# A query projection split around the first cross-attention scores, with an order of its own for ScalarE, in a two-layer decoder trunk

## The reference, cut to what matters

```
def memory_cross_attention(h, mem_n, wq, wkv, qn_g, kn_g, wo):
    B, S, _ = h.shape
    q = rmsnorm((h @ wq).reshape(B, S, XA_HEADS, XA_HEAD_DIM), qn_g)
    k, v = jnp.split(mem_n @ wkv, 2, axis=-1)
    k = rmsnorm(k.reshape(B, MEM_LEN, XA_HEADS, XA_HEAD_DIM), kn_g)
    ...
    s = jnp.einsum("bshd,bmhd->bhsm", q, k).astype(jnp.float32) * (XA_HEAD_DIM ** -0.5)
    p = jax.nn.softmax(s, axis=-1)
    o = jnp.einsum("bhsm,bmhd->bshd", p.astype(v.dtype), v).reshape(B, S, D_MODEL)
    return o @ wo
```

## Time and profile before

| what | us |
|---|---|
| median of 3 runs | 1440.24 (1438.99 to 1440.38) |
| profiled execution | 1440.78 |
| its span, first to last instruction | 1439.0 |
| TensorE matmul busy | 1149.5 (80%) |
| TensorE weight load busy | 565.2 (39%) |
| DVE busy | 326.0 (23%) |
| ScalarE busy | 199.1 (14%) |
| GpSimd busy | 46.0 (3%) |
| DMA, mean over the span | 332 GB/s |

### The profile page before, as it was taken

One profiled execution on the slowest core, in us unless ns is written; L12 is line 12 of the kernel. 1 busy time (PEld: TensorE's weight loads), 2 busy tenths in 40 slices (PEclk: granted clock), 3 DMA queues, 4 the chain that ended last, 5 costly groups with the idle time before them and its releaser, 6 DMA issues.

```text
span 1439.0 us, 14402 instructions
## 1 busy us (share of the span) xinstructions
PE 1149.5 (80%) x5938; PEld 565.2 (39%) x5938; DVE 326.0 (23%) x843; ACT 199.1 (14%) x460; POOL 46.0 (3%) x87
## 2 busy tenths in 40 slices
PE   8999999997868666685879999989956756667576
PEld 5775555553223222231325776456312212122121
DVE  2126543132022010110102286223201101011011
ACT  3034313110101000000002252121000000000000
POOL 1010010000000000000001100100000000000000
PEclk9999999998989888997989999999988888888889
DMA  9663363379999999999998345534999999999997
GB/s 373 218 234 117 143 266 118 119 285 423 426 426 426 428 422 427 428 427 425 427 426 313 119 176 199 210 118 177 415 427 427 426 427 426 428 427 428 427 428 305
DMA packets 90771, 477.97 MB, mean 332 GB/s; under 512 B 4342, under 2 KB 10958, under 8 KB 41038
## 3 DMA queue, kind: packets, MB, share of 16 engines
q1 hardware_dynamic: 89783, 475.25, 81.0%
q10 hardware_dynamic: 919, 1.74, 0.3%
HBM read 475.92 MB, written 1.05 MB: 331 GB/s over the span
## 4 chain that ended last, share of the span: by engine, by line
PE 54%; DMA 39%; DVE 4%; issue 1%; SPq 1%; ACT 1%; POOL 0%; DVEq 0%; ACTq 0%; POOLq 0%
PE bank L1438 51%; DMA ring<-exp_w 37%; PE bank L1445 2%; SPq L568 1%; DMA conv_mem<-memT 1%; DVE fox_ssd L1196 0%; DVE SCO L1034 0%; DVE SCO L1189 0%; DMA con<-const 0%; DVE gate_in L1328 0%; ACT SCO L748 0%; DVE Y L1287 0%; DVE X L1042 0%; DVE Y L1282 0%; DVE keys_values L976 0%
## 5 line engine op out<-in xcount | busy, mean ns | idle before, releaser
L1438 PE MATMUL bank<-ring,proj_ht 128*32 128x512 f32 (+3 forms) x2496 | 451.6, 669 | 157.5 <-DMA ring<-exp_w 156.4
L1438 PEld LDWEIGHTS bank<-ring,proj_ht 128*32 128x32 f32 (+1 forms) x2496 | 169.5, 141 | 395.3 <-issue 376.7
L1438 PE MATMUL bank<-ring,SCO 128*32 128x512 f32 x928 | 136.5, 699 | 63.3 <-DMA ring<-exp_w 54.3
L1438 PE MATMUL bank<-ring,H 128*128 128x512 f32 x256 | 112.5, 593 | 0.0
L1042 DVE TENSOR_TENSOR X<-X,bank 128x512 f32<-128x512 f32 x64 | 44.0, 687 | 294.4 <-PE bank L1438 294.4
L1438 PE MATMUL bank<-proj_ht,H 128*128 128x128 f32 x512 | 76.2, 302 | 33.2 <-DVE proj_ht L1002 26.6
L1438 PEld LDWEIGHTS bank<-proj_ht,H 128*128 128x128 f32 x512 | 66.7, 207 | 72.0 <-DVE proj_ht L1002 36.8
L1438 PEld LDWEIGHTS bank<-ring,SCO 128*32 128x32 f32 x928 | 36.9, 125 | 147.6 <-issue 131.5
L1034 DVE SCALAR_TENSOR_TENSOR SCO<-Y,bank 128x512 f32<-128x512 f32 x16 | 17.1, 1068 | 287.3 <-PE bank L1438 287.3
L1438 PEld LDWEIGHTS bank<-ring,H 128*128 128x128 f32 x256 | 47.9, 190 | 55.7 <-issue 55.0
L1438 PE MATMUL bank<-fox_ssd,proj_ht 128*128 128x512 f32 x128 | 59.1, 604 | 0.0
(11 more groups left out here) (220 smaller groups left out, 825.4 us busy)
## 6 DMA issues: line engine op xcount, KB each, us to landing
ring<-exp_w SPq DMA_DIRECT2D x182, 2048.0 KB, 20.5
ring<-w_in SPq DMA_DIRECT2D x8, 2048.0 KB, 19.1
ring<-xa_wkv SPq DMA_DIRECT2D x4, 2048.0 KB, 7.8
ring<-w_out SPq DMA_DIRECT2D x4, 2048.0 KB, 7.7
ring<-xa_wq SPq DMA_DIRECT2D x4, 2048.0 KB, 7.7
ring<-xa_wo SPq DMA_DIRECT2D x4, 2048.0 KB, 7.9
ahead<-xa_wkv SPq DMA_DIRECT2D x4, 2048.0 KB, 26.5
ring<-w_in SPq DMA_DIRECT2D x6, 1024.0 KB, 12.8
```

Of the source, the lines that this page charges most:

```text
L1438: return nc.tensor.matmul(dst, lhsT, rhs, start=start, stop=stop)
```

## The change

Three things change, in both layers:

1. TensorE does the first four chunks of the projection (1,1), then the scores of heads 0 and 1 of tile 0 and the transposes `("qT", 1, 0)`, and then the other four chunks (`"q rest"`). The jobs behind it are in a new order, in which both transposes `xpT` of a head mostly stand one `xo` ahead of their use. The planner takes `CROSS_PE` without `"q rest"`, so some banks differ.
2. ScalarE has a list of its own, `CROSS_ACT`. In it the exponentials of heads 0 and 1 of tile 0 come before the take of the projection (1,1), and the exponential `("xs", 1, 0)` comes behind two copies of transposes.
3. DVE's list is changed to match: the copy `("qT", 1, 0)` goes before the first share, the norm (1,1) goes behind the maxima and the share of heads 2 and 3, and the share of head 3 of tile 0 moves to near the end.

```
-CROSS_PE = [("qT", 0, 0), ("qT", 0, 1), ("q", 1, 1), ("xs", 0, 0), ("xs", 0, 1), ("qT", 1, 0), ("xs", 0, 2),
...
+CROSS_PE = [("qT", 0, 0), ("qT", 0, 1), ("q", 1, 1), ("xs", 0, 0), ("xs", 0, 1), ("qT", 1, 0), ("q rest",), ("xs", 0, 2),
+            ("xs", 0, 3), ("xs", 1, 0), ("xpT", 0, 0), ("xpT", 0, 1), ("qT", 1, 1), ("xs", 1, 1), ("xs", 1, 2),
+            ("xpT", 1, 0), ("xs", 1, 3), ("xpT", 1, 1), ("xo", 0), ("xpT", 0, 2), ("xpT", 1, 2), ("xo", 1),
+            ("xpT", 0, 3), ("xpT", 1, 3), ("xo", 2), ("out2", 0, 0), ("xo", 3)]
+CROSS_ACT = [("xs", 0, 0), ("xs", 0, 1), ("q rest",), ("xs", 0, 2), ("xs", 0, 3), ("xpT", 0, 0), ("xpT", 0, 1),
+             ("xs", 1, 0), ("xs", 1, 1), ("xpT", 1, 0), ("xs", 1, 2), ("xpT", 1, 1), ("xs", 1, 3), ("xo", 0),
+             ("xpT", 0, 2), ("xpT", 1, 2), ("xo", 1), ("xpT", 0, 3), ("xpT", 1, 3), ("xo", 2), ("xo", 3)]
...
+             ("qT", 1, 0), ("share", 0, 0), ("share", 0, 1), ("max", 0, 2), ("max", 0, 3), ("share", 0, 2),
+             ("norm", 1, 1), ("max", 1, 0), ("qT", 1, 1), ("max", 1, 1), ("share", 1, 0), ("max", 1, 2),
+             ("share", 1, 1), ("max", 1, 3), ("share", 0, 3), ("share", 1, 2), ("share", 1, 3)]
...
-                for job in CROSS_PE:
-                    if job[0] == "q":
+                for job in CROSS_ACT:
+                    if job[0] == "q rest":
                         take_q(1, 1)
...
-            def tile_job(l, job, w, t, lhs):
+            def tile_job(l, job, w, t, lhs, chunks=range(KC)):
...
-                last.then_inc(filled(l, job), 1)
+                if chunks[-1] == KC - 1:
+                    last.then_inc(filled(l, job), 1)
...
                     if job[0] == "q":
-                        query(1, 1)
+                        query(1, 1, range(4))
+                    elif job[0] == "q rest":
+                        query(1, 1, range(4, KC))
```

More of the change, by code:

```diff
@@ L96 @@
 AFTER_CB = [("kv", 3, 1), ("in", "z1", 1)]
-CROSS_PE = [("qT", 0, 0), ("qT", 0, 1), ("q", 1, 1), ("xs", 0, 0), ("xs", 0, 1), ("qT", 1, 0), ("xs", 0, 2),
-            ("xs", 0, 3), ("qT", 1, 1), ("xs", 1, 0), ("xs", 1, 1), ("xpT", 0, 0), ("xpT", 1, 0), ("xs", 1, 2),
-            ("xpT", 0, 1), ("xo", 0), ("xs", 1, 3), ("xpT", 1, 1), ("xpT", 0, 2), ("xo", 1), ("xpT", 1, 2),
-            ("xpT", 0, 3), ("xo", 2), ("xpT", 1, 3), ("out2", 0, 0), ("xo", 3)]
+CROSS_PE = [("qT", 0, 0), ("qT", 0, 1), ("q", 1, 1), ("xs", 0, 0), ("xs", 0, 1), ("qT", 1, 0), ("q rest",), ("xs", 0, 2),
[5 more added lines that the diff above has]
+             ("xpT", 0, 2), ("xpT", 1, 2), ("xo", 1), ("xpT", 0, 3), ("xpT", 1, 3), ("xo", 2), ("xo", 3)]
 CROSS_DVE = [("norm", 0, 0), ("norm", 1, 0), ("qT", 0, 0), ("qT", 0, 1), ("norm", 0, 1), ("max", 0, 0), ("max", 0, 1),
-             ("share", 0, 0), ("qT", 1, 0), ("norm", 1, 1), ("max", 0, 2), ("share", 0, 1), ("max", 0, 3),
-             ("share", 0, 2), ("qT", 1, 1), ("max", 1, 0), ("share", 0, 3), ("max", 1, 1), ("share", 1, 0),
-             ("max", 1, 2), ("share", 1, 1), ("max", 1, 3), ("share", 1, 2), ("share", 1, 3)]
+             ("qT", 1, 0), ("share", 0, 0), ("share", 0, 1), ("max", 0, 2), ("max", 0, 3), ("share", 0, 2),
+             ("norm", 1, 1), ("max", 1, 0), ("qT", 1, 1), ("max", 1, 1), ("share", 1, 0), ("max", 1, 2),
+             ("share", 1, 1), ("max", 1, 3), ("share", 0, 3), ("share", 1, 2), ("share", 1, 3)]
 MAXIMA = [_job[1:] for _job in CROSS_DVE if _job[0] == "max"]
@@ L141, in list_jobs @@
     jobs += [("ysT", t) for t in range(NT)]
-    jobs += two("hT2", 0) + [("q", 0, 0)] + two("hT2", 1) + [("q", 1, 0), ("q", 0, 1)] + CROSS_PE
+    jobs += two("hT2", 0) + [("q", 0, 0)] + two("hT2", 1) + [("q", 1, 0), ("q", 0, 1)] + [job for job in CROSS_PE if job != ("q rest",)]
     jobs += [("out2", 1, 0), ("out2", 0, 1)] + two("xT", 0) + [("out2", 1, 1), ("router",)] + two("xT", 1)
@@ L1453, in arrived @@
                 return ring_view(i % SLOTS, IN_COLS.get(unit[0], (0, 512))[1])
-            def tile_job(l, job, w, t, lhs):
-                pe.wait_ge(*free(l, job))
-                for c in range(KC):
+            def tile_job(l, job, w, t, lhs, chunks=range(KC)):
+                if chunks[0] == 0:
+                    pe.wait_ge(*free(l, job))
+                for c in chunks:
                     last = mm(bk(l, job)[:, 0:w.shape[2]], lhs[:, t, c, :], w[:, c, :], start=c == 0, stop=c == KC - 1)
-                last.then_inc(filled(l, job), 1)
+                if chunks[-1] == KC - 1:
+                    last.then_inc(filled(l, job), 1)
             def transpose_keys(l, n, t):
@@ L1792, in transpose_q, with query @@
                     transposes(l, ("qT", t, i), [Q_tm[:, t, (4 * i + j) * P:(4 * i + j + 1) * P] for j in range(4)])
-                def query(n, t):
-                    tile_job(l, ("q", n, t), arrived(l, ("wq", n)), t, HT)
+                def query(n, t, chunks=range(KC)):
+                    tile_job(l, ("q", n, t), arrived(l, ("wq", n)), t, HT, chunks)
                 both_copied("hT2", 0)
```

## The result

| | before | after |
|---|---|---|
| median, us (5 runs each, same chip) | 1440.24 (1438.99 to 1440.42) | 1433.69 (1431.78 to 1434.35) |
| profiled execution, us | 1440.78 | 1431.97 |
| its span, us | 1439.0 | 1430.2 |

The changed kernel takes 0.9949 of the time before (95% interval 0.9939 to 0.9960): 6.55 us less between the medians, where 10.3 were forecast. (The ratio of the two medians alone is 0.9955; the recorded ratio, 0.9949, would be 7.3 us of 1440.24.) Lines of the changed kernel stand three higher than before (L1441 was L1438, L984 was L981).

What follows compares the result with a forecast made beforehand. The expert stage's length is fixed by its bytes, its start hangs on TensorE getting through the cross-attention. Two layers by 5.16 us give 10.3, router clock 0, so 1440.24 falls to 1429.9, said as 1430.0; 80% range 1427.5 to 1434.

Steps and rivals of the forecast that it cites:

- forecast as walked: Whole kernel: the main case, 1428 to 1432 us, chance 0.72.
- 80% range: Whole kernel: 1427.5 to 1434 us, the upper end set with the case of a falling clock.
- The walk through the cross-attention: Cross-attention: new order priced job by job from old rows, 256.23 against 261.39 us, 5.16 us less for each layer.
- the likeliest rival: Cross-attention: TensorE's clock falls in the new order too, 1.7 us a layer, 1431.6 or 1433.3 us; chance 0.13.
- only the 2.08 us wait brought it down: Old cross-attention: argument against the clock rival; the 1.34 us wait before xo 1 left the clock at 1.00.
- The waits have one origin: Old cross-attention, 6.7 us lost: ScalarE handles projection (1,1) before any exponential, so all scores are packed behind it.
- no gain: Expert stage: quad 0 waits for a load that didn't move up; 1440 us, chance 0.04.
- slower: Cross-attention: clock falls in the gap at 243.4 and stays low until its end; 1454 us, chance 0.03.
- a new wait in the cross-attention: A wait the walk doesn't see, for instance norm (1,1) held on DVE, takes half; 1434 to 1436 us, chance 0.06.
- the router's clock: Router fillers, mostly at 1.2 GHz: a clock falling elsewhere gives or takes about 0.7 us a layer; estimate 0.
- A second term: Old cross-attention: 1.7 us of each layer's 5.2 us gain is the low clock, the rest waits.

Runs made afterwards that it cites:

- the split alone: Kernel before with projection (1,1) in two halves and ScalarE following TensorE, TensorE's and DVE's jobs in the old order: 1442.80 us, ratio 1.0017.
- all but the split: The change with projection (1,1) whole at its old place and its take first on ScalarE: 1434.77 us, ratio 0.9957.
- second and third trace: The changed kernel run again unchanged, twice: 1433.32 us, ratio 0.9952, and 1432.45 us, ratio 0.9950.
- the changed kernel with its gap filled: The change plus two filler matmuls in the wait before the second router group, all 10 fillers kept: 1429.53 us, ratio 0.9927.
- six fillers: The changed kernel with 6 instead of 10 filler matmuls before the ranking of the experts: 1430.59 us, ratio 0.9936.
- the version with the take first: The change with the take of projection (1,1) put back ahead of the exponentials on ScalarE: 1435.56 us, ratio 0.9975.

## Why the prediction came out as it did

**Where the measured time lies.** 1433.69 us is outside "forecast as walked" (1428 to 1432, 0.72) and 0.3 us inside the 80% range (to 1434). The room up to 1434 was made for a clock that falls in the new cross-attention. That did not happen; the time came from another place, the router. That the range held is luck in this respect.

**The walk through the cross-attention was right.** Forecast 29.0 to 29.1 us a layer, measured 29.20 in six layers of three traces. Forecast waits of 1.0 us before qT (1,1) and 0.4 before xpT (1,0), none before xo 1 and xo 2: measured 241.58 - 240.57 = 1.0, 0.4 and none. First exponential forecast at 233.2, measured 233.67 with the stage starting 0.43 later. The load into keys_values forecast near 256.5, measured 257.11. The clock of 1.00 held, so the likeliest rival (the clock falls here too, 0.13) did not occur. Its argument against, that "only the 2.08 us wait brought it down", does not hold as a rule: in three of eight layers of the old order the same wait left the clock at 1.00. The Trainium skill (TensorE: Matmul & The Clock Gate, "A second HAM failure mode: psum-queue depth-cycling", the section behind the one that the prediction names) tells of a bf16 kernel, cycling through PSUM banks, in which short idles between groups of matmuls made the clock fall and rise again. This case is in float32. No layer of the changed kernel's cross-attention shows it (29.20 us and 1.00 each time); five of eight layers of the old order do, and so does the router around its wait of 1.02 us.

**The origin of the waits was named wrong.** The prediction says: "The waits have one origin. ScalarE handles the query projection (1,1) before any exponential". Two experiments speak against it. With the exponentials ahead and the jobs in their old order (the split alone), the waits of 1.92, 1.17 and 0.56 us are all still there, 34.32 us. With the take first as in the kernel before and the jobs in the new order (all but the split), the first is down to 0.5 us and the others are gone, 29.62 us. So the order of the jobs behind the projection carries 4.63 of the 5.05 us. ScalarE's order matters only once the projection is split: then the take first costs 1.9 us a layer. The walk came out right all the same, because it went job by job through the whole new order and didn't use the one origin.

**The expert stage moved up.** The time from the ring load of layer 0 to layer 1's cross-attention is 619.98 before and 619.13 after, 619.49 and 619.44 in the second and third trace: the rival "no gain" (0.04) is out. So are "slower" and a new wait in the cross-attention: the only waits there are the two forecast.

**The step that failed is the router's clock:** "a clock that falls elsewhere gives back at most 0.7 us a layer, or takes about as much. Estimate: 0". What it can give back was right: 44.62 us at full clock in the changed kernel with its gap filled, 0.64 below 45.26. What it can take was too small. It was read from a single low stretch of 3.4 us, most of it under fillers. These ended at 298.11, already 0.8 us behind the choice of experts (297.32), so whatever more they take counts in full; in the changed kernel the stretch is 6.8 us long, which loses 1.7 us more at half rate: +1.6 us in five of six layers. The term was set at 0, both ends ±0.7, and measured +1.13 us a layer on average (46.62 less 45.49, below).

**A second term was right in size but perhaps not in certainty:** 1.7 us of each layer's gain were the low clock of the earlier trace rows, which the forecast took as a fixed part of the kernel before. Three of eight layers of the old order don't have it; 34.25 - 32.57 = 1.68 us is its price. None of these three is a layer of the unchanged kernel before.

**Put together.** The router stretch averages 45.49 us in four layers of the kernel before and 46.62 in six of the changed one, which takes 1.13 a layer or 2.3 from the 10.1 us of the cross-attentions. Left are 7.8 us. If the old cross-attention has its low clock in only five layers of eight, its average is (5 x 34.25 + 3 x 32.57)/8 = 33.62, the gain there 4.42 a layer, and 6.6 us are left. The median difference was 6.55 us, and the three ratios (0.9949, 0.9952, 0.9950) stand for 6.9 to 7.3. So the router term is needed; whether the second is, these few traces can't tell.

**Open** is why the low stretch at the router is mostly 6.8 us in the changed kernel and 3.4 us in the kernel before. Code there is the same, and the same kernel shows either length. The traces show where the stretch fell, not what places it. One thing goes with it over all fourteen traces, whose routers differ in part: in the six layers in which the clock had fallen in the cross-attention, the router's stretch was 3.4 us; of the 22 others, thirteen had 6.8, eight 3.4 and one none. Layer 0 of the split alone, with the old order but a clock of 1.00 in its cross-attention, had 46.92 us. So part of what the change gains by not having the low clock ahead may come back here. That is an observation; no run tests it. The length of the router stretch with six fillers (45.06 and 45.32 against mostly 46.9) shows that the fillers matter in the changed kernel, but not that the change must always meet the worse case: the version with the take first had 45.25 and 45.24.

## What to carry to other kernels

Walk the new order with prices of the old trace, job by job and engine by engine; it gave a stage of 29 us to 0.2 us. It doesn't say which of several edits made together carries the gain. For that, undo them one at a time: here it was the order of jobs, not the split and not the early exponentials. But a low-clock stretch in one profile is one draw: before it is entered as a gain, or its effect elsewhere as zero, take two or three traces, and ask what work lies under it, since low clock under fillers costs little as long as they end before the engine that the path waits for, and under a quad's first matmuls it costs in full. After a change upstream, filler counts deserve a new try: four fewer were worth 2 to 3 us in the new kernel, by overlapping intervals, and nothing in the old.

## What the runs showed of the hardware

- The same code with the same four waits to 0.01 us (0.38, 1.91, 1.17 and 0.56 us) ran through the same stretch at a granted clock of 1.00 in one trace (32.57 us) and with a part at 0.50 in another (34.25 us). A wait of about 2 us in itself does not decide it: the split alone had waits of 2.13 and 1.92 us in layer 0 and took 34.32 us, 0.07 more than before, with over 1.7 us more of waiting.
- The low stretches at the router lasted 3.4 or about 6.8 us in 27 of the 28 layers traced, never a length between; one layer had none. Those in the cross-attention (six layers) all lasted 3.4 us.
- The low level's price depends on what lies under it. The first quad's matmuls took 2.05 us at full clock and 2.79 to 3.79 with the low one on them, all of it on the path; under the fillers of the kernel before it cost 0.64 us (45.26 against the 44.62 of the changed kernel with its gap filled, at full clock). In layer 1 of the split alone 3.4 us of low clock cost 0.2 us, since they ate into a wait.
